# Four batches' value pages in turn: a new order of page matmuls in the decode attention of a hybrid decoder step

## The reference

```python
k_prev = cache_k[j][page_table].reshape(Bs, PAST_LEN, H_A, DH_A)   # 8 batches, 8 pages of 128 keys each
v_prev = cache_v[j][page_table].reshape(Bs, PAST_LEN, H_A, DH_A)
...
p = jax.nn.softmax(s.reshape(s.shape[:3] + (-1,)), axis=-1).reshape(s.shape)
return jnp.einsum('bqhjk,bqhjkd->bqhd', p, vg.astype(F32)).astype(q.dtype)
```

## Time and profile before

| | us |
|---|---|
| three runs | 957.46, 958.67, 960.42 |
| median | 958.67 |
| span of the profiled execution | 959.2 |
| TensorE busy in it | 883.4 |
| VectorE, ScalarE, GpSimd busy | 622.1, 420.1, 257.4 |

### The profile page before, as it was taken

One profiled execution on the slowest core, in us unless ns is written; L12 is line 12 of the kernel. 1 busy time (PEld: TensorE's weight loads), 2 busy tenths in 40 slices (PEclk: granted clock), 3 DMA queues, 4 the chain that ended last, 5 costly groups with the idle time before them and its releaser, 6 DMA issues.

```text
span 959.2 us, 16875 instructions
## 1 busy us (share of the span) xinstructions
PE 883.4 (92%) x6145; PEld 761.0 (79%) x6145; DVE 622.1 (65%) x943; ACT 420.1 (44%) x695; POOL 257.4 (27%) x226
## 2 busy tenths in 40 slices
PE   2999894969999999999999999969969999999996
PEld 1988783742325999999999999857648999999995
DVE  3689988660032798888556656565476888887442
ACT  4434333341011565555545433564334655555442
POOL 6154767710100332232001000161221332222010
PEclk9999996588999999999999999975597999999997
DMA  9837675335565555554556667403353566653631
GB/s 275 284 129 242 199 260 183 128 94 160 192 220 175 176 177 175 178 184 129 172 177 192 191 187 216 161 10 100 88 155 93 171 192 188 188 157 121 183 119 46
DMA packets 154406, 159.83 MB, mean 167 GB/s; under 512 B 11793, under 2 KB 136349, under 8 KB 154335
## 3 DMA queue, kind: packets, MB, share of 16 engines
q1 hardware_dynamic: 145520, 151.09, 50.6%
q10 hardware_dynamic: 7966, 6.33, 2.2%
q0 software_dynamic: 864, 1.68, 0.7%
HBM read 150.76 MB, written 8.50 MB: 166 GB/s over the span
## 4 chain that ended last, share of the span: by engine, by line
PE 81%; DVE 11%; ACT 4%; issue 2%; DMA 2%; ACTq 0%; POOL 0%; SPq 0%; DVEq 0%
PE bank L1396 20%; PE bank L1397 20%; PE bank L1398 20%; PE bank L1604 6%; DVE w_lo L921 3%; DVE sc_all L973 2%; PE bank L1773 1%; PE bank L1726 1%; DMA z<-in_c_out_norm_g 1%; PE bank L1485 1%; PE bank L1600 1%; PE bank L1566 1%; PE bank L1748 1%; PE bank L1737 1%; DVE z L968 1%
## 5 line engine op out<-in xcount | busy, mean ns | idle before, releaser
L530 ACT ACTIVATE w_hi<-w_raw 128x1024 fp32r<-128x1024 f32 (+2 forms) x230 | 227.9, 993 | 297.8 <-PE bank L1398 294.5
L921 DVE TENSOR_TENSOR w_lo<-w_raw,w_hi 128x1024 fp32r<-128x1024 f32 (+2 forms) x230 | 296.1, 1289 | 83.6 <-ACT w_hi L530 83.4
L1396 PE MATMUL bank<-actB_hi,w_hi 128*128 128x264 f32 x704 | 200.1, 284 | 0.0
L1397 PE MATMUL bank<-actB_lo,w_hi 128*128 128x264 f32 x704 | 199.5, 283 | 0.0
L1398 PE MATMUL bank<-actB_hi,w_lo 128*128 128x264 f32 x704 | 199.3, 283 | 0.0
L1396 PE MATMUL bank<-actA_hi,w_hi 128*128 128x264 f32 x624 | 184.8, 296 | 5.8 <-DVE w_lo L921 2.9
L1397 PE MATMUL bank<-actA_lo,w_hi 128*128 128x264 f32 x624 | 180.1, 289 | 0.0
L1398 PE MATMUL bank<-actA_hi,w_lo 128*128 128x264 f32 x624 | 179.8, 288 | 0.0
L1397 PEld LDWEIGHTS bank<-actB_lo,w_hi 128*128 128x128 f32 x704 | 132.6, 188 | 0.1
L1396 PEld LDWEIGHTS bank<-actB_hi,w_hi 128*128 128x128 f32 x704 | 132.6, 188 | 0.1
L1398 PEld LDWEIGHTS bank<-actB_hi,w_lo 128*128 128x128 f32 x704 | 132.0, 187 | 0.0
(11 more groups left out here) (326 smaller groups left out, 1191.2 us busy)
## 6 DMA issues: line engine op xcount, KB each, us to landing
w_raw<-in_ffn_w SPq DMA_DIRECT2D x44, 1024.0 KB, 5.3
kv<-in_cache_k SPq DMA_DIRECT2D x64, 256.0 KB, 3.0
kv<-in_cache_v SPq DMA_DIRECT2D x64, 256.0 KB, 3.1
w_raw<-in_c_w_in SPq DMA_DIRECT2D x16, 1024.0 KB, 5.6
w_raw<-in_ab_w_in SPq DMA_DIRECT2D x14, 1024.0 KB, 5.4
w_raw<-in_ffn_w SPq DMA_DIRECT2D x16, 768.0 KB, 4.5
w_raw<-in_ffn_w SPq DMA_DIRECT2D x16, 640.0 KB, 4.1
w_raw<-in_ab_w_out SPq DMA_DIRECT2D x4, 1024.0 KB, 5.7
```

What stands on the lines that cost most here:

```text
L530: A(whi[u % RING][:, 0:nk, :], raw[u // 2 % RING][:, 0:nk, P * (u % 2):P * (u % 2) + P], ACT.Copy).then_inc(sem("hi_ready"), 1)
L921: V.tensor_tensor(wlo[u % RING][:, 0:nk, :], raw[u // 2 % RING][:, 0:nk, P * (u % 2):P * (u % 2) + P], whi[u % RING][:, 0:nk, :].bitcast(F ...
L1396: M(bank[b][:, 0:T], hi[:, k, :], src[0][:, k0 + k, :], start=first and k == 0, stop=False)
L1397: M(bank[b][:, 0:T], hi[:, k, :], src[1][:, k0 + k, :], start=False, stop=False)
```

## The change

The 64 value pages are taken in two windows `w` of four batches. Within a window the order is page by page and, for each page number `g`, batch by batch `q`, so that four matmuls in a row write four 32-row slices of one bank. The four own-value matmuls of a window come first. The ring holds the same eight pages, but each is issued, used and freed singly: page `i` waits for `v_used` at `i - 7`, one increment a page. TensorE still waits for two pages at a time. SyncE loads the page numbers of four batches (32) at the head of each window. The retention work keeps its order, one part after each group of four pages: a state update after groups 0 to 3, two readouts after groups 4 to 7, one `ret_squares` after groups 8 to 11. VectorE waits for 64 increments in place of 32.

```diff
--- before.py
+++ after.py
@@ -225,6 +225,10 @@
         vec_rows = zf[0:52, 3200:3328]
         cw_rows = [zf[0:88, 3328 + 128 * l:3456 + 128 * l] for l in range(2)]
         cb_rows = [zf[0:88, 3584 + 512 * l:4096 + 512 * l].rearrange("p (q n) -> p q n", q=4) for l in range(2)]
+        def v_page(i):
+
+            return kv[i % 8 // 2][:, i % 2, :]
+
         ident = cst[:, C_ID:C_ID + P]
         perm = cst[:, C_PERM:C_PERM + P]
         bones = cst[:, C_BONES:C_BONES + P]
@@ -310,9 +314,19 @@
                 k_pages(13 + 2 * n)
             for j in range(20, 32):
                 k_pages(j)
-            for j in range(32):
-
-                page_pair(j, cache_v, (sem("k_reduced"), 29 + j) if j < 4 else (sem("v_used"), j - 3))
+            for w in range(2):
+                rows = [nc.values_load_multi_w_load_instructions(
+                    pg[0:1, 8 * (4 * w + q):8 * (4 * w + q) + 8], engines=[mybir.EngineType.SP], min_val=0, max_val=NPOOL - 1)[1]
+                    for q in range(4)]
+                for g in range(NPAGE):
+                    for q in range(4):
+                        i = 32 * w + 4 * g + q
+                        if i < 8:
+                            sp.wait_ge(sem("k_reduced"), 29 + i // 2)
+                        else:
+                            sp.wait_ge(sem("v_used"), i - 7)
+                        sp.dma_start(v_page(i), cache_v[0, bass.ds(rows[q][g], 1)].rearrange("o p h d -> p (o h d)")
+                                     ).then_inc(sem(f"kv_landed{i % 8 // 2}"), 16)
 
             def ffn_loads(l, u_up, u_dn):
                 def pair(n, c, i8):
@@ -1107,7 +1121,7 @@
                 V.tensor_tensor(actA[1][:, 4 + c, :], z0[:, c, :], actA[0][:, 4 + c, :].bitcast(F32), ALU.subtract
                                 ).then_inc(sem("mix_lo"), 1)
 
-            dve.wait_ge(sem("v_used"), 32)
+            dve.wait_ge(sem("v_used"), 64)
             for t in range(2):
                 V.tensor_tensor(ovv[:, t, :].rearrange("p (h d) -> p h d", h=H), bank[6 + t][:, :].rearrange("p (h d) -> p h d", h=H),
                                 cst[:, C_HMASK:C_HMASK + 8].unsqueeze(2).to_broadcast([P, H, DA]), ALU.mult).then_inc(sem("samp_own"), 1)
@@ -1593,22 +1607,24 @@
             claim(7, "samp_own", 2)
             pe.wait_ge(sem("own_p_diag"), 1)
             pe.wait_ge(sem("samp_pt_out"), 1)
-            for j in range(32):
-                b, r = j // 4, 32 * (j // 4 % 4)
-                out = bank[6 + b // 4][r:r + H, :]
-                if j % 4 == 0:
-                    M(out, dgp[:, b, :], tks["va"][:], start=True, stop=False)
-                pe.wait_ge(sem(f"kv_landed{j % 4}"), 32 * (8 + b + 1))
-                for t in range(2):
-                    g = 2 * (j % 4) + t
-                    ins = M(out, pts[:, g, 8 * b:8 * b + 8], kv[j % 4][:, t, :], start=False, stop=g == NPAGE - 1)
-                ins.then_inc(sem("v_used"), 1)
-                if j < 4:
-                    state_update(4 + j)
-                elif 5 <= j < 13:
-                    ret_o((j - 5) // 4, (j - 5) % 4)
-                elif 15 <= j < 19:
-                    ret_squares(j - 15)
+            for w in range(2):
+                for q in range(4):
+                    M(bank[6 + w][32 * q:32 * q + H, :], dgp[:, 4 * w + q, :], tks["va"][:], start=True, stop=False)
+                for g in range(NPAGE):
+                    for q in range(4):
+                        i, b = 32 * w + 4 * g + q, 4 * w + q
+                        if q % 2 == 0:
+                            pe.wait_ge(sem(f"kv_landed{i % 8 // 2}"), 32 * (8 + i // 8 + 1))
+                        M(bank[6 + w][32 * q:32 * q + H, :], pts[:, g, 8 * b:8 * b + 8], v_page(i),
+                          start=False, stop=g == NPAGE - 1).then_inc(sem("v_used"), 1)
+                    n = 8 * w + g
+                    if n < 4:
+                        state_update(4 + n)
+                    elif n < 8:
+                        ret_o((n - 4) // 2, 2 * (n % 2))
+                        ret_o((n - 4) // 2, 2 * (n % 2) + 1)
+                    elif n < 12:
+                        ret_squares(n - 8)
             claim(5, "mix_lo", 5)
             pe.wait_ge(sem("samp_own"), 2)
             for t in range(2):
```

## The result

The changed kernel takes 937.15 us (median of 4 runs, 934.67 to 953.46) against 958.13 (4 runs, 957.46 to 960.42) for the kernel before, a ratio of 0.973 with a 95% interval of 0.9689 to 0.9772. The profiled execution took 937.78, with a span of 936.0 where before it was 959.2. So 21 us went at the median and 23.2 between the two profiled executions, against 11.7 forecast.

The account below looks back on a forecast made before the run. It took TensorE's page matmuls, 0.87 us a page, to bound the value stage. Ending that stage at 284.2 instead of 298.5 gains 14.3, less 2.5 behind it: 11.8 off 959.2 gives 947.4, said as 947 us, range 936 to 957.

Parts of the forecast that it names:

- Overlap of four: Value stage, TensorE: four pages in different slices cost 0.87 us together at 2.4 GHz, 1.67 at 1.2 GHz.
- second and third rivals: Value stage: second, four streams share, 3.49 us a group, 957.5 to 960, chance 0.10; third, halves block, 2.2, 942, 0.08.
- The fourth: Rival, value stage: halves hold each other back at 1.2 GHz, 4.4 us a group; 30 slower, 989; chance 0.08.
- The pages late next: Value stage: page transfers bound next, 0.85 us a page after 1.7 lead; DMA share near 0.9 in the second half.
- Groups 0 to 3: Value stage's first four page groups: with state updates of 1.1 us each fitting in, group 4 starts at 232.7.
- The loads of the second window: SyncE, value stage: 32 page numbers take 10.2 us, so page 32 leaves at 252.2; TensorE's readouts cover most.
- The clock: TensorE, value stage: 2.4 GHz until group 3, 1.2 GHz after, because it waits for pages in nearly every group.
- The 2.5 us that were to be lost behind the stage: Behind the value stage at 1.2 GHz: weight loads 1.6 us more, output projection 0.9 more.
- The first rival: Value stage: overlap with the clock kept at 2.4 GHz, end at 280.7, 17.8 us less, 941; chance 0.22.
- The stage: Value stage as a whole: ends at 284.2 instead of 298.5, a gain of 14.3 us.
- The retention tail: VectorE and ScalarE after the last squares, 9.7 us: stays hidden by 4 us or so.
- The end of the sum: Whole kernel: 14.3 gained less 2.5 lost is 11.8 us, taking the span from 959.2 to 947.4.

Follow-up runs that it names:

- one_slice: Changed kernel with all four batches of a window written to one 32-row slice, against the kernel before: 966.5 us, ratio 1.0047.
- early: Changed kernel with the second window's page-number loads spread out and retention work moved ahead, against the kernel before: 942.31 us, ratio 0.9674.
- after_shift: Changed kernel with the last eviction before the mLSTM stage made five times, to start that stage about 2.3 us later: 942.77 us.
- after_hold2: Changed kernel with 21 extra unread matmuls in three TensorE waits at the mLSTM stage's head, against the kernel before: 926.70 us, ratio 0.9629.
- after_again: Changed kernel rerun without an edit on a second chip, against the kernel before: 947.82 us, ratio 0.9828.
- after_hold: Changed kernel with 17 extra unread matmuls in three TensorE waits at the mLSTM stage's head, against the kernel before: 932.85 us, ratio 0.9677.
- before_hold: Kernel before with 17 extra unread matmuls in three TensorE waits at the mLSTM stage's head: 964.06 us.

## Why the prediction was right in its way and wrong in its size

*Overlap of four: right.* The timeline of TensorE after, for 220.2 to 220.6 (start, length, what):

```profile
220.25 1.04 PE L1618 MATMUL bank<-kv,pts 128*8 128x512 f32 x4
```

Four of the group's eight matmuls have started by 220.6, and from the first start to the last end the four take 1.04; the other four, each page's second, start from 221.06 on. The earlier trace rows shows two such streams; here are four. The second and third rivals fall with it: shared streams would have left one_slice and the kernel after alike (they are 85.86 and 67.76), and halves that hold each other back would have made a group five halves of 0.83 (half of the 1.67 of a lone page at 1.2 GHz), 4.2 us, where 1.82 were measured. The fourth falls too: the clock was at 1.2 GHz in the first half of the stage, and a group stayed at about 2.

Different slices alone are not enough, though. The prediction says of the kernel before that nothing there shows two slices side by side; but the first own-value matmul of a batch (8 rows by 8 columns) goes to another slice than the last page of the batch ahead of it (128 rows), and the timeline of TensorE before shows these two one behind the other:

```profile
283.53 7.03 PE L1604 MATMUL bank<-kv,pts 128*8 128x512 f32 x16
290.49 1.02 PE L1600 MATMUL bank<-tks_va,dgp 8*8 8x512 f32 x2
291.44 7.03 PE L1604 MATMUL bank<-kv,pts 128*8 128x512 f32 x16
```

The own-value matmul starts at 290.49, 0.07 before the pages' 16 matmuls end at 290.56. Neighbours of one shape overlap in the kernel after, four pages and four own values alike; why this pair did not is open.

The rule of the Trainium skill that the prediction set against this ("TensorE: Matmul & The Clock Gate", section "Part 3: Packing small matmuls — row/col tiling"), that matmuls start and end strictly in program order, is again not what the trace shows. By that rule the group would be the 4.2 just worked out. The same section gives 2.38 as the speed-up of three column tiles; here four have 4 x 1.67 / 1.82 = 3.7.

*The pages late next: right.* After 258 the DMA share is 0.86 and 0.97 and TensorE waits. Page 32 left at 255.69 and the stage ended 30.5 us later; the sum had 28.9 + 1.4 + 1.7 = 32.0, of which the 1.4, 0.2 for handing over a slot, rested on no row. early, with less in front of the pages, has a DMA share of 0.87 or more from 230 on, but TensorE is without a gap until 260 there too.

*Groups 0 to 3: 1.4 us too short.* Group 4 began at 235.66, not 232.7; 1.6 of this is the later start. The rest is that I priced a state update at its 2.4 GHz time of 1.1, and it ran at 1.2 GHz and took 1.89, so that four pages and an update came to 3.7 to 3.9.

*The loads of the second window: right.* 10.4 us against 10.2, page 32 at 255.7 against 252.2 (the 3.0 from above, and 0.5), the share in the hole 0.16, and the readouts over it: two took 3.50 at 1.2 GHz, where 3.8 were taken.

*The clock: wrong in order, right in sum for the stage.* I had 2.4 GHz until group 3 and 1.2 after. It was 1.2 GHz from 211.7, ahead of the stage, to 266.3, and then 2.4 GHz in a stretch where TensorE worked 10.89 of 16.20 us. So waiting for pages did not cost it the clock in this profile, and work without a gap did not bring it back: from 228 to 258 TensorE has none, at 1.2 GHz throughout. In after_shift and after_hold2, with the same value stage, the clock did fall between page waits, at 277.1 and at 274.4. The 2.5 us that were to be lost behind the stage did not come in after: mask to projection takes 3.87 in both. In after_hold2 and early, 1.2 and 1.6 of them do come. The first rival, 941 with the clock kept, is nearer to the median for another reason than its own.

*The stage: right.* 13.9 us shorter, 14.3 forecast, in part by luck: the stage ended 2.0 later than the sum had it, from 1.6 of later start, 1.4 and 0.5 too little up to page 32 and 1.5 too much behind it. Across the profiles it takes 81.65 to 87.2 where one batch's pages or one slice fill it, 66.6 to 70.4 where four slices do and the loads and the retention work stand as in the change.

*The retention tail: right.* VectorE's last squares come at 274.12 and its tail still ends ahead of the mask, as the timeline of VectorE of the kernel after shows (start, length, what, and in brackets the idle time before it and for what):

```profile
274.12 0.43 DVE L1112 TENSOR_SCALAR z<-bank 128x264 f32<-128x264 f32 x1 [4.29 <-PE bank L1589]
...
282.39 1.46 DVE L1121 TENSOR_TENSOR actA_lo<-z,actA_hi 128x264 fp32r<-128x264 f32 x4
286.19 1.29 DVE L1126 TENSOR_TENSOR tok_kb<-bank,cst 128x512 f32<-128x512 f32 x2 [2.34 <-PE bank L1618]
```

In answer to the earlier trace rows, 2.34 us of cover are left, where about 4 were foreseen.

*The end of the sum: the step that failed.* "Net: 14.3 - 2.5 = 11.8. The span is 959.2; 959.2 - 11.8 = 947.4." This takes all behind the output projection as only shifted. The mLSTM stage is not of one length: 1.2 GHz held there for 61.4 us in the profile of before, the longest stretch of all the profiles, for 41.0 in that of after, and for 58.0 in after_again, the same kernel. With no long low stretch the stage takes 70.2 (70.1 in after_hold), with 20.5 us of it 72.6, with 41.0 84.3, with 51.2 87.8 to 93.1, with 58.0 to 61.4 94.0 or so. So of the 23.2 between the profiles 9.7 are this stage, near its slowest in the one and middling in the other. Against the forecast span of 947.4 the profiled 936.0 is 11.4 less: 9.7 in the mLSTM stage and 1.2 behind it, both at nothing in the sum, and 2.5 of loss that stayed away, less the 2.0 by which the value stage ended later. The start of the value stage moves in the same way, 214.7 to 223.8, with 41.0 to 58.0 us at 1.2 GHz in the attention ahead of it. What the change does by itself is 14.7 with the clock of the mLSTM stage held, and 16.5 on the chip on which its mLSTM stage took 94.1; the forecast of 11.7 is 3 short of that, 2.5 of it the loss behind the stage that mostly stayed away. The other 6 of the first 21 are of the size that the low stretches, in stages that the change doesn't touch, give or take between profiles; that they came of that alone is not shown.

What sets the length of a low stretch is open. A shift of the start did not steer it. That it varies in an unchanged kernel and that matmuls in the waits hold the clock is shown; why the first four runs of the changed kernel had 935 to 938 three times and the six of after_again 945 to 948 is not. Nor is it shown that the change has no part in it. Without the extra matmuls the changed kernel stood 21.0 below the kernel before, 20.3 (after_shift) and 16.5 (after_again), each time more than 14.7; and the kernel before stayed within 957.46 to 968.80 in all its 45 runs, while these 14 of the changed one go from 931.78 to 953.59.

## What to carry to other kernels

Where several products have few output rows, give neighbours of one shape in the program different 32-row slices of the accumulator: here TensorE worked on four of them at once, and the transfers then have to be looked at as the next bound, with the instructions on the issuing queue between them. Before a sum is carried to the end of a kernel, look for stages behind the change where the clock is at its low level: in this kernel their length was not fixed, and a difference between two profiles there says nothing on the change until the clock is held alike in both, or the kernel is run again elsewhere.

## What the runs showed of the hardware that I had not expected

- Four 32-row slices run nearly at four times the rate of one even with 128 rows of fp32 moving data: 1.82 us for four pages against 3.33 for two, both at 1.2 GHz. A matmul of 8 rows in another slice, behind one of 128, started only 0.07 us before that one's end.
- The low stretches of the clock differ between executions of one kernel, 41.0 and 58.0 us in the mLSTM stage. A low us costs 0.12 to 0.45 there: (72.6 - 70.2) / 20.5 in after_shift, (84.3 - 70.2) / 41.0 = 0.34 in after, (93.1 - 70.2) / 51.2 in before_hold.
- 21 matmuls of 128x256 whose results nobody reads, in three waits, bring up to 24 us in the mLSTM stage (94.0 to 70.2) and 19 us of the kernel before (960.73 to 941.43). With 17 of them the clock still fell in the profile of before_hold.
- Eight page numbers cost SyncE 2.6 us (10.4 for 32), more than its issue of seven pages (0.33 each).
